# A chunked recurrence on three engines: the order of the work at a turn's edge is changed on TensorE, VectorE and ScalarE, and the buffers' first filling is moved on GpSimd

## What is computed

```
def step(s, inp):
    r_t, w_t, k_t, v_t, a_t, b_t = inp
    sa = einsum('bhvk,bhk->bhv', s, a_t)
    s = s * w_t[:, :, None, :] + sa[..., :, None] * b_t[:, :, None, :] + v_t[..., :, None] * k_t[:, :, None, :]
    return s, einsum('bhvk,bhk->bhv', s, r_t)
...
wl = -softplus(-(w0 + tanh(xw) @ w_up)) - 0.5      # decay
a = sigmoid(a0 + xa @ a_up)                        # learning rate
kd = k * (1 + (a - 1) * k_a)
y, s = wkv_scan(s0, r, decay, kd, v, -kk, kk * a, rev)
```

## Time and profile before

| what | value |
|---|---|
| median of 3 timed runs | 2306.35 us (2301.39 to 2307.17) |
| the profiled execution, its own time | 2300.42 us |
| span of its trace | 2298.6 us |
| PE busy | 2064.5 us (90%) |
| DVE busy | 1564.1 us (68%) |
| ACT busy | 1258.4 us (55%) |
| POOL busy | 658.5 us (29%) |
| the recurrence | from 394.5 to about 830 us of the span |
| r0 of turn 0 to r0 of turn 19 | 449.69 to 819.98 us, 19 turns |
| a turn without a hitch, outputs included | about 19.4 us |

### The profile page before, as it was taken

One profiled execution on the slowest core, in us unless ns is written; L12 is line 12 of the kernel. 1 busy time (PEld: TensorE's weight loads), 2 busy tenths in 40 slices (PEclk: granted clock), 3 DMA queues, 4 the chain that ended last, 5 costly groups with the idle time before them and its releaser, 6 DMA issues. The chain is left out here.

```text
span 2298.6 us, 48388 instructions
## 1 busy us (share of the span) xinstructions
PE 2064.5 (90%) x20142; PEld 1641.8 (71%) x20142; DVE 1564.1 (68%) x2248; ACT 1258.4 (55%) x2319; POOL 658.5 (29%) x469
## 2 busy tenths in 40 slices
PE   5999998589999988990999999999959999999989
PEld 3788887477887743770788788888747778866667
DVE  4566664789998746326799989999766846556531
ACT  5422221577777654442788888888545434367530
POOL 0000020566676500205032322323034455400011
PEclk9999999799999989995999999999979999999999
DMA  8222261223333158426699999999745364340032
GB/s 290 58 69 65 68 160 31 55 56 72 72 72 72 44 191 295 148 92 247 255 353 397 385 383 389 380 400 390 252 146 169 106 223 120 85 133 2 2 116 77
DMA packets 163493, 397.82 MB, mean 173 GB/s; under 512 B 13630, under 2 KB 57036, under 8 KB 163276
## 3 DMA queue, kind: packets, MB, share of 16 engines
q1 hardware_dynamic: 148780, 346.48, 43.0%
q0 software_dynamic: 12096, 44.05, 6.9%
q10 hardware_dynamic: 2400, 4.21, 0.5%
HBM read 346.98 MB, written 46.14 MB: 171 GB/s over the span
## 5 line engine op out<-in xcount | busy, mean ns | idle before, releaser
L1998 DVE TENSOR_TENSOR exp_w_lo<-mixT,exp_w_hi 128x2048 fp32r<-128x2048 f32 x124 | 279.0, 2288 | 22.8 <-ACT exp_w_hi L1955 22.7
L1955 ACT ACTIVATE exp_w_hi<-mixT 128x1024 fp32r<-128x1024 f32 x256 | 255.0, 1052 | 57.9 <-PE banks L1917 34.5
L2211 POOL TENSOR_TENSOR w_lo<-mixT,w_hi 128x512 fp32r<-128x512 f32 (+1 forms) x108 | 144.9, 1363 | 164.8 <-ACT w_hi L2287 162.0
L1917 PE MATMUL banks<-exp_w_hi,xsT_lo 128*128 128x512 f32 x512 | 161.1, 396 | 5.9 <-DVE xsT_lo L2002 5.9
L1917 PE MATMUL banks<-exp_w_lo,xsT_hi 128*128 128x512 f32 x512 | 159.4, 393 | 0.0
L1917 PE MATMUL banks<-exp_w_hi,xsT_hi 128*128 128x512 f32 x512 | 158.8, 391 | 0.0
L1885 POOL DMA_INDIRECT moe_rows<-exp_out,idxT x16 | 25.1, 1571 | 438.6 <-DVE exp_out L2057 438.6
L2269 PE MATMUL banks<-w_hi,h_lo 128*128 128x512 f32 (+1 forms) x320 | 122.6, 383 | 7.8 <-POOL w_lo L2211 5.3
L1870 POOL DMA_INDIRECT xs<-xn_rows,idxT x16 | 116.0, 7253 | 12.8 <-DVE idxT L2029 4.3
L2269 PE MATMUL banks<-w_lo,h_hi 128*128 128x512 f32 (+1 forms) x320 | 119.6, 374 | 0.0
L2269 PE MATMUL banks<-w_hi,h_hi 128*128 128x512 f32 (+1 forms) x320 | 119.4, 373 | 0.0
(11 more groups left out here) (401 smaller groups left out, 5737.5 us busy)
## 6 DMA issues: line engine op xcount, KB each, us to landing
mixT<-in_exp_w_up_dram SPq DMA_DIRECT2D x62, 1024.0 KB, 10.4
mixT<-in_exp_w_gate_dram SPq DMA_DIRECT2D x34, 1024.0 KB, 9.8
mixT<-in_exp_w_down_dram SPq DMA_DIRECT2D x32, 1024.0 KB, 9.1
mixT<-in_w_in_dram SPq DMA_DIRECT2D x96, 256.0 KB, 2.9
ada_w_second<-in_ada_w_dram SPq DMA_DIRECT2D x16, 1024.0 KB, 9.7
kaT<-in_exp_w_down_dram SPq DMA_DIRECT2D x16, 1024.0 KB, 7.1
exp_w<-in_exp_w_down_dram SPq DMA_DIRECT2D x16, 1024.0 KB, 7.6
kaT<-in_exp_w_gate_dram SPq DMA_DIRECT2D x15, 1024.0 KB, 10.9
```

What stands on the lines that cost most here:

```text
L1917: mm = pe.matmul(g.ps[bank + q][:, :], lhs[:, kk, :], wide[:, k, q * 512:(q + 1) * 512], start=(kk == 0 and p == 0), stop=(kk == KT - 1 an ...
L1955: last = act.activation(wh[:, n % RH, k, :], w[n % RING][:, k, :], ACT.Copy)
L1998: dve.tensor_tensor(wl[:, n % RH, :, :], w[n % RING], wh[:, n % RH, :, :], ALU.subtract).then_inc(lo_ok, 1)
L2211: pool.tensor_tensor(wl[:, q % SR, 0:width(q)], w[:, q % WR, 0:width(q)], wh[:, q % SR, 0:width(q)], ALU.subtract).then_inc(w_lo, 1)
```

## The change

On each of three engines pieces are named in another order, one wait is split off, and one piece of POOL's work is moved from ahead of the loop into it. Nothing is added to the arithmetic or taken from it.

```
@@ POOL
-            (zero the state, zero w, copy the unit matrix into w_last)      # ahead of the loop
+            def fixed_parts(): (the same instructions)
...
                 if inside(h + 2):
                     key(h + 2)
                     end_block(h + 2)
+                if h == -2:
+                    fixed_parts()
@@ ACT
             def decay_rate(s):
                 act.wait_ge(logits_ok[s % 2], th(s))
-                step(act.activation(v.sw, v.sw, ACT.Tanh, scale=0.5))
+                act.activation(v.sw, v.sw, ACT.Tanh, scale=0.5).then_inc(decay_tanh[s % 2], 1)
+
+            def one_added(s):
+                act.wait_ge(decay_tanh[s % 2], th(s))
                 act.activation(v.sw, v.sw, ACT.Identity, bias=g.c("one")).then_inc(tanh_w[s % 2], 1)
...
             for h in TURNS:
+                if inside(h + 2):
+                    decay_rate(h + 2)
                 if inside(h - 1):
                     take_r0(h - 1)
-                if inside(h + 2):
-                    decay_rate(h + 2)
                 if inside(h):
                     turned(h, 1)
+                if inside(h + 2):
+                    one_added(h + 2)
                 if inside(h - 1):
                     take_v(h - 1)
@@ DVE
-            dve.wait_ge(zeroed, 2)
             for h in TURNS:
+                if h == 0:
+                    dve.wait_ge(zeroed, 2)
...
-                if inside(h):
-                    level(h, LAST)
                 if inside(h + 3):
                     logits(h + 3)
                 if inside(h + 2):
                     feature_b(h + 2)
+                if inside(h):
+                    level(h, LAST)
@@ PE
-            pe.wait_ge(zeroed, 2)
             for h in TURNS:
+                if h == 0:
+                    pe.wait_ge(zeroed, 2)
...
                 if inside(h):
                     join(h, 1)
+                if inside(h + 1):
+                    products(h + 1)
                 if inside(h - 1):
                     apply_last(h - 1)
-                if inside(h + 1):
-                    products(h + 1)
...
                 if inside(h + 1):
                     gram(h + 1, 3)
+                if inside(h + 3):
+                    logits(h + 3)
                 if inside(h):
                     z(h, LAST)
-                if inside(h + 3):
-                    logits(h + 3)
                 if inside(h):
                     r0(h)
```

More of the change, by code:

```diff
@@ L767, in _, with fixed_parts @@
             eye = g.c("eye").unsqueeze(1)
[L768 to L778, removed]
-            pool.wait_ge(halved, 1)
+            pool.wait_ge(halved, 1)
+            def fixed_parts():
+                for d in range(2):
+                    ins = pool.memset(group[0].sv[d][HALVES[d], :, :], 0.0)
+                ins.then_inc(zeroed, 1)
+                pool.wait_ge(zeroed, 1)
+                for v in group:
+                    pool.memset(v.w[:, :, :, :, :], 0.0)
+                    for e in range(2):
+                        kept = slice((1 - e) * HC, (2 - e) * HC)
+                        ins = pool.tensor_copy(v.last[:, e, :, kept], eye[:, :, kept].to_broadcast([P, HP, HC]))
+                ins.then_inc(zeroed, 1)
+                pool.wait_ge(zeroed, 2)
             def fade(s):
@@ L895, in decay_rate, with one_added @@
                 act.wait_ge(logits_ok[s % 2], th(s))
-                step(act.activation(v.sw, v.sw, ACT.Tanh, scale=0.5))
+                act.activation(v.sw, v.sw, ACT.Tanh, scale=0.5).then_inc(decay_tanh[s % 2], 1)
+            def one_added(s):
+                v = group[s % 2]
+                act.wait_ge(decay_tanh[s % 2], th(s))
                 act.activation(v.sw, v.sw, ACT.Identity, bias=g.c("one")).then_inc(tanh_w[s % 2], 1)
```

11 lines of the change are left out of this document (7 added, 4 removed).

## The result

| what | before | after |
|---|---|---|
| median of 12 timed runs each | 2307.35 us | 2318.47 us |
| ratio after / before, 95% interval | | 1.0057 [1.0046, 1.0068] |
| the profiled execution, its own time | 2300.42 us | 2313.92 us |
| span of its trace | 2298.6 us | 2312.1 us |
| end of the projection ahead of the recurrence | 394.50 | 396.75 |

The kernel became 0.57% slower by the ratio of the timed runs (the medians stand 0.48% apart); the forecast was 2310.9 us, 0.20% slower than the 2306.35 on which it was built, with a range of 2302 to 2318. One of the 12 executions of before took 4056.21 us, and the ratio leaves it out. The start won 4.9 us (forecast 3.05) and the recurrence lost 16.7 us (forecast 7.6).

What follows compares the result with a forecast made beforehand. Busy shares name PE; at the edge it waits 0.77 us for ACT at join 1, with three chains close at join 2. Recurrence +7.6 and start -3.05 give +4.5 us, 2310.9 on the timed median; range 2302 to 2318.

Steps and rivals of the forecast that it cites:

- The start: First logits no longer wait for POOL's filling: -3.1 us, +0.45 for slowed feature_k, -0.4 for faster matmuls, together -3.05.
- the recurrence: All turns together lose 7.6 us, with bounds of +2 and +11.
- a regular turn: One turn of the recurrence becomes about 0.35 us longer, between +0.1 and +0.5; summed for nine turns at 0.37.
- the turns with a hitch: Eight of 18 turns with late level-1 transposes pass the delay to the sums and join 2: +0.5 us each, 4.0 together.
- Logits wait for the end columns: At the edge, logits ahead of z start 0.09 us earlier, PE idles before them, r0 comes 0.23 later.
- "The stall comes back whole from DVE and PE.": At join 1, ACT's 0.77 us stall goes, but level 1's masking on DVE holds join 1 at 607.80 against 607.81.
- "Nothing else waits for apply_inverse but v's copy.": apply_inverse starts at 606.99 instead of 606.34, behind the last level's masking, and only v's copy waits for it.
- products ahead of apply_last: After join 1, apply_last and u's copy come later, so join 2 starts at 612.52 against 612.14, +0.38 us.
- The first: Rival: the stall goes and nothing replaces it, join 1 0.6 us earlier in 17 turns; -13 us, 2293; chance 0.07.
- The second: Rival: z of the last level passes the waiting logits inside PE, r0 not delayed; -1.5 us, 2305; chance 0.15.
- The third: Rival: clearly slower, late transposes, slowed feature_b and the edge cost more, filling slows DVE; +8 to +9, 2315; chance 0.28.
- feature_k and the memset: At the start, feature_k beside POOL's moved filling is slowed, +0.45 us; by the skill page it would not be.

Runs made afterwards that it cites:

- after_twice: The changed kernel with the first logits' 32 small matmuls issued twice on PE; ratio to before 1.0060 [1.0042, 1.0079].
- dve_edge_only: Before, with only DVE's last-level masking moved behind logits and feature_b, PE's order kept; ratio to before 1.0050 [1.0031, 1.0068].
- fill_twice: Before, with POOL's filling moved and the first logits' 32 small matmuls issued twice; ratio to before 1.0006 [0.9993, 1.0018].

## Why the prediction was wrong, step by step

The direction and the mechanism of a regular turn were right. Two terms of the sum failed: the size of a regular turn, 0.70 us instead of 0.37, and the turns with a hitch, which I took as they stood before while the stops doubled and turns 0 to 3 lost 6.9 us. Over the 13 turns of the image the first is all of their +9.1 us. All steps are counted from the end of ACT's end columns, 602.68 before and 610.08 (609.63 + 0.45) after.

| step | forecast | measured |
|---|---|---|
| logits start | +0.05 | +0.14 |
| r0 starts | +1.62 | +1.67 |
| DVE takes the logits | +1.25 | +1.36 |
| level 1's masking ends | +5.08 | +5.16 |
| join 1 starts | +5.12 | +5.32 |
| u's copy starts, from join 1 | 2.19 | 2.31 |
| join 2 starts, from u's copy | 2.53 | 2.52 |
| join 2 starts | +9.84 | +10.15 |

- **Logits wait for the end columns.** Right in kind: PE idles 0.58 and ACT ends it. The forecast took 0.05 from an ACT end to PE, as at join 1. For this pair it was 0.14 before as well (602.68 to 602.82), and I had put that down to z in front. The row showed the price and I argued it away.
- **"The stall comes back whole from DVE and PE."** Right, and more than whole. Join 1 stands 0.16 behind DVE's masking; the forecast used 0.04. The row was there: before, the masking for level 2 ended at 612.00 and join 2 started at 612.14, the later of its two inputs 0.14 ahead of it, and I had quoted both without using the difference. apply_inverse shows the same 0.15 (614.48 to 614.63). Together the two latencies make the 0.20 by which join 1 is later than forecast.
- **"Nothing else waits for apply_inverse but v's copy."** Wrong as a statement, since join 1 is queued behind it on PE and v's copy ahead of join 1's on ACT; but it cost nothing here, because 614.63 + 0.61 (its 32 matmuls, as from join 1 to products) is 615.24, ahead of the masking's arrival at 615.40. With the last masking ahead of feature_b, apply_inverse stops waiting and join 1 gains 0.32 behind r0, which is 0.2 of a turn (19.88 against 20.12). What serves join 1 there is the shorter path of DVE: feature_b took 1.18 instead of 1.50.
- **products ahead of apply_last.** Right: +0.5 us alone, and u's copy 2.31 behind join 1, forecast 2.19. The last levels' 32 matmuls end a little later than one length behind products.
- **Turns with a hitch.** I took the hitches as they were, 8 turns at +0.5. They grew from 8.5 to 17.6 us in all, and what they were was unknown to me. In the image they cost no more than before, so 0.5 a turn stands where the regular 0.70 was paid. Turns 1 to 3 took 4.45 us more, and with the pieces shifted (after_twice) 0.7 more, so most of it goes with the stops. Turn 0 took 2.5 us more, with 2.3 us of stops in it and none before. The sum was off by 9.1 us: 4.3 by the regular turn's size in the image (13 x 0.70 against 13 x 0.37), and 4.8 in the other turns, above all 0 to 3, for which the forecast leaves 7.6 - 4.8 = 2.8 us and which took 7.6.
- **The start** was better than forecast, 4.9 against 3.05, and part of that is luck. The wait gave 3.17; the logits at 2.4 instead of 1.2 GHz let DVE begin 0.85 earlier behind PE's start (1.29 instead of 2.14), where I had put 0.4; the first of the running sums' halves took 0.68 instead of 1.34 (403.81 before); and feature_k was not slowed (0.45 not paid). The three profiles of the same start in which these logits ran mostly at the lower clock won 3.1 to 4.2 us, the forecast's 3.05 at their lower end.
- **The rivals.** The first (the stall goes whole) fell. The second (z passes the waiting logits) fell: z starts at 611.17, 0.95 behind the first of them. The Trainium skill, page TensorE: Matmul & The Clock Gate, section "The mechanism", has matmuls keep their order strictly; here the trace agrees. By that rule the few records of apply_last ahead of products' last (616.88) would be a matter of logging, as the earlier trace rows; no run tests this. The third has the sign, and its deciding point, 0.55 us a turn, was passed, but not for its reasons: the turns that had hitches before cost no more than others, and DVE was not slowed by the filling at the start.
- **feature_k and the memset.** 0.68 us next to a memset of 1.07, as alone. The Trainium skill, page SBUF — State Buffer, section "Who interferes with whom", says that a VectorE instruction with two SBUF inputs contends with a GpSimd instruction that reads SBUF and not with one that only writes it. For the memset the trace agrees.

What stays open: whether TensorE's clock falls in turn 0 in every execution of the kernels whose profile shows it, and what makes it fall there and in some starts; what asks for the next piece of the program, and so at which places it is late; and why the timed ratio of dve_edge_only (1.0050) is above what its one profile shows (2306.3 us against a median of 2315.1).

## What to carry to other kernels

A stall that one engine ends tells how late that engine is, not how much is won when it is early: read when the other inputs of the same instruction arrive, and move a piece only if all of them have room. Here DVE's masking was ready 0.28 us before ACT's copy, and the new order made it 0.36 us later (5.16 against 4.80 behind the end columns). In a chain of short pieces, read the latency of each wait from a row of just that wait, not only of that pair of engines: from ACT's end to PE's start it was 0.05 at the joins and 0.14 at the logits, from DVE's end to join 1 0.16. Two of them made 0.2 of the 0.3 us by which the turn was missed. And a barrier that only the later turns need belongs to them: moving the filling was the one part that paid, 0.21%, and that kernel has the lowest ratio of those run. In fill_twice, with the doubled logits and the lower clock at the start, nothing of it was left (1.0006).

## What the runs showed of the hardware

- TensorE waits for its own program. With small matmuls starting every 14 to 30 ns (z's 32 within 0.44 us, r0's within 0.93), the 127 that belong to one 16 KB piece of instructions ran in as little as 2.5 us (from 466.5 in after), while in none of the 15 profiles did two pieces land less than 3.2 us apart. Where PE outran them it stopped, for 0.3 to 1.9 us, in the trace "issue". In the image's turns of after, which have waits of their own, the added stops were mostly hidden. 128 instructions more at the start move all of them to other places.
- With its pieces shifted, the same order of work differed by 5.9 us over turns 1 to 18 (after and after_twice, one profile each), 0.26% of the kernel. An effect of that size needs a second run with the program shifted, compared stretch by stretch.
- After 5.93 us of idle time the first 128 logits of the recurrence ran at a granted clock of 0.50 to 0.56 (3.44 to 3.69 us) in all six kernels that had it and no doubling. After 2.76 us they ran at 1.00 in three kernels (2.10 us) and at 0.53 to 0.59 in three (3.23 to 3.59 us), with the same program on PE up to there. So one profile of a start says little about its clock. A stop or a wait can cost more than its length: in after_twice ten us of gram parts at 0.50 followed a stretch with a stop in which PE was busy for 2.71 of 5 us. In after PE was busy for 3.66 of 5 us and the clock stayed at 1.00.
